# Moving half blocks of dense work within a written-out tensor-engine order: attention scores, and the tiles of a chunked recurrence

## The reference, cut to what matters

```
h   = RMSNorm(x);  c = h @ w_in            # RWKV-7 columns, attention q|k|v, two gates
A   = RWKV-7 time mixing of c              # matrix-state recurrence, 8 heads of 64
Bd  = differential attention               # softmax(q1 k1) - lam*softmax(q2 k2), times v
mix = sigmoid(gA)*(A @ w_out_a) + sigmoid(gB)*(Bd @ w_out_b)
x   = x + RMSNorm(mix @ w_o)
x   = x + RMSNorm(SwiGLU(RMSNorm(x) @ w_ffn_in) @ w_ffn_out)
```

## Time and profile before

| | |
|---|---|
| median of 3 runs | 1002.26 us (1001.57 to 1004.27) |
| the profiled execution's own time | 1004.91 us |
| its span, first to last instruction | 1003.1 us |
| busy | PE 96%, PEld 91%, POOL 55%, DVE 45%, ACT 29% |
| mean granted TensorE clock | 0.996 of 2.4 GHz |
| attention, 190 to 324 us | PE busy 130.66 of 134 us |
| recurrence, 324 to 480 us, tiles 0 to 3 | PE busy 34.78 of 39, 34.62 of 38, 35.76 of 39, 35.97 of 40 us |

### The profile page before, as it was taken

How to read it: one execution, slowest core, us unless ns; L and a number is a source line. 1 busy time by engine, 2 the same in 40 slices (tenths; PEclk the granted TensorE clock), 3 DMA queues, 4 the chain that set the end, 5 groups by cost and what they waited for, 6 DMA issues and landing times.

```text
span 1003.1 us, 23249 instructions
## 1 busy us (share of the span) xinstructions
PE 959.4 (96%) x9424; PEld 910.9 (91%) x9424; DVE 450.6 (45%) x870; ACT 290.3 (29%) x828; POOL 549.9 (55%) x595
## 2 busy tenths in 40 slices
PE   5999999999999899889999989999999999999996
PEld 4999899988878787778899989999999999999996
DVE  5456688467744445455466653333333333100003
ACT  5225265245564233432313541111111111111101
POOL 6667899634354243243469325555555555656671
PEclk9999999999999999999999999999999999999998
DMA  8333322332223111150046322223322223223232
GB/s 252 93 86 84 85 63 72 114 109 76 78 67 93 39 47 35 55 208 28 28 122 217 94 64 63 84 85 91 95 84 84 84 85 96 81 80 95 80 95 90
DMA packets 138306, 89.76 MB, mean 89 GB/s; under 512 B 5514, under 2 KB 130160, under 8 KB 138224
## 3 DMA queue, kind: packets, MB, share of 16 engines
q1 hardware_dynamic: 129604, 73.17, 25.7%
q10 hardware_dynamic: 8620, 15.42, 4.3%
HBM read 79.39 MB, written 9.19 MB: 88 GB/s over the span
## 4 chain that ended last, share of the span: by engine, by line
PE 86%; DVE 6%; ACT 4%; POOL 2%; issue 2%; DMA 1%; ACTq 0%; DVEq 0%; SPq 0%; POOLq 0%
PE dense L1069 71%; PE side L1149 3%; PE side L1192 1%; PE side L1218 1%; POOL w_lo L770 1%; PE side L1270 1%; PE side L977 1%; PE side L910 1%; DMA xs<-in_x_prompt 1%; PE side L896 1%; POOL w_hi L765 1%; PE side L951 1%; DVE gain L1731 1%; DVE h_lo L1724 0%; PE side L1242 0%
## 5 line engine op out<-in xcount | busy, mean ns | idle before, releaser
L765 POOL TENSOR_SCALAR w_hi<-w_raw 128x256 fp32r<-128x256 f32 (+1 forms) x255 | 155.6, 629 | 348.7 <-PE dense L1069 331.1
L770 POOL TENSOR_TENSOR w_lo<-w_raw,w_hi 128x256 fp32r<-128x256 f32 (+1 forms) x255 | 323.0, 1288 | 9.8
L1069 PE MATMUL dense<-h_hi,w_hi 128*128 128x272 f32 (+2 forms) x1376 | 297.8, 295 | 2.9 <-DVE h_lo L1724 1.5
L1069 PE MATMUL dense<-h_hi,w_lo 128*128 128x272 f32 (+2 forms) x1376 | 289.3, 289 | 0.0
L1069 PE MATMUL dense<-h_lo,w_hi 128*128 128x272 f32 (+2 forms) x1376 | 288.4, 288 | 0.0
L1069 PEld LDWEIGHTS dense<-h_hi,w_hi 128*128 128x128 f32 x1376 | 217.8, 189 | 12.4 <-issue 6.9
L1069 PEld LDWEIGHTS dense<-h_lo,w_hi 128*128 128x128 f32 x1376 | 218.4, 189 | 0.0
L1069 PEld LDWEIGHTS dense<-h_hi,w_lo 128*128 128x128 f32 x1376 | 217.4, 189 | 0.0
L1069 PE MATMUL dense<-S,w_hi 128*128 128x272 f32 (+2 forms) x648 | 109.3, 289 | 0.0
L1069 PEld LDWEIGHTS dense<-S,w_hi 128*128 128x128 f32 x648 | 92.1, 188 | 0.3 <-issue 0.2
L1069 PE MATMUL dense<-S,w_lo 128*128 128x272 f32 (+2 forms) x324 | 68.2, 288 | 0.0
(11 more groups left out here) (286 smaller groups left out, 1345.4 us busy)
## 6 DMA issues: line engine op xcount, KB each, us to landing
w_raw<-in_w_ffn_in SPq DMA_DIRECT2D x44, 512.0 KB, 3.8
w_raw<-in_w_in SPq DMA_DIRECT2D x43, 512.0 KB, 3.9
w_raw<-in_w_ffn_out SPq DMA_DIRECT2D x16, 448.0 KB, 3.7
gates<-gst ACTq DMA_DIRECT2D x16, 272.0 KB, 2.1
w_raw<-in_w_ffn_out SPq DMA_DIRECT2D x8, 512.0 KB, 3.8
w_raw<-in_w_out_a SPq DMA_DIRECT2D x5, 512.0 KB, 3.5
w_raw<-in_w_o SPq DMA_DIRECT2D x5, 512.0 KB, 4.5
mb<-gates ACTq DMA_DIRECT2D x1, 2176.0 KB, 9.2
```

The source lines that it names most:

```text
L765: ins = nc.gpsimd.tensor_scalar(hi[:, q], raw[:, q], 1.0, 0.0, ALU.mult, ALU.add)
L770: ins = nc.gpsimd.tensor_tensor(lo[:, q], raw[:, q], hi[:, q].bitcast(F32), ALU.subtract)
L1069: ins = pe.matmul(acc[:, bk, 0:tn], w, r[:, t0:t0 + tn], start=first and n == 0, stop=final and n == 2)
```

## The change

In attention the third piece of a head group is drawn as before, but where a group has scores (`attS`, i + 2 still in range) it goes ahead of them and behind the second piece. In the recurrence two fillers of each of the tiles 0 to 3 move: the one behind `sk` and `xi` goes ahead of `sk`, behind the transposes of `tok`; the one behind `e` goes ahead of `e`, behind `wu`. The number of pieces and what each computes are the same; tile 4 is as it was.

```diff
     for i, th in enumerate(heads):
         rows = [piece() + [("attP", *th)], piece()]
+        third = piece()
         if i + 1 < len(heads):
             rows[-1] += [("attC", *heads[i + 1])]
         if i + 2 < len(heads):
-            rows[-1] += [("attS", *heads[i + 2])]
-        rows += [piece() + [("attO", *th)] + ([("vtok", th[0] + 1)] if th[0] < SAMPLE and th[1] == 1 else [])]
+            rows[-1] += third + [("attS", *heads[i + 2])]
+            third = []
+        rows += [third + [("attO", *th)] + ([("vtok", th[0] + 1)] if th[0] < SAMPLE and th[1] == 1 else [])]
...
-        s += both("sb0", t + 1) + both("tok", t) + both("sk", t) + both("xi", t + 1) + filler(1) + scores
-        s += both("wu", t) + both("e", t) + filler(1) + yfin
+        s += both("sb0", t + 1) + both("tok", t) + filler(1) + both("sk", t) + both("xi", t + 1) + scores
+        s += both("wu", t) + filler(1) + both("e", t) + yfin
```

## The result

The changed kernel takes 1010.3 us (median of 20 runs, 1005.62 to 1016.01), the kernel before 1003.88 beside it (20 runs, 1001.57 to 1008.1): ratio 1.0066, 95% interval 1.0053 to 1.0078. It is slower by 0.66%, clear of the noise. The forecast was 1004.8 us, no difference (range 1001 to 1008). The profiled execution took 1009.32 us (span 1007.5, clock 0.994) against 1004.91 (span 1003.1, clock 0.996).

A forecast was written before the change was run, and what follows sets the result against it. The prediction took PE to bound the kernel (86% of the chain that ended last). Recurrence +1.45 us and attention +1.1 us gave +2.55 us on the median of 1002.26, so 1004.8 us, range 1001 to 1008.

The forecast's parts named there:

- I carry the difference over to the median: Whole kernel: terms counted on the profiled 1004.91 us were added to the three runs' median, 1002.26, lying 2.65 us lower.
- The clock falls once more: Rival, slower: one more stretch at 1.2 GHz, 1.7 us lost, total +4.3 us, 1006.5; chance 0.13.
- Tile 1 and tile 0: Recurrence: `sb1` g1 starts later because DVE runs `xi` ahead of `rb`'s mask; +0.95 us in tile 1, +0.5 in tile 0.
- The next thing late is DVE, and its queue holds `xi`: Recurrence, tile 1: `xi`, 1.60 us on DVE, delays `sb1` g1; cost +1.01 us net of the gain at `sk`.
- the split that delays `xi`: Rival, tile 0: POOL's split begins late and delays `xi`; +3.0 instead of +0.5 us, 1007.3 in all; chance 0.08.
- Behind `wu`: Recurrence, tile 1: 0.5 us saved at `e`, some 0.4 us of new waiting at `pre0`; -0.07 us.
- term for tile 2: Recurrence, tile 2: the delay from `sb1` is swallowed by the wait at the block's end; -0.1 us.
- Tile 3: Recurrence: `sb1` g1 is 0.64 us later, but most of it vanishes in PE's 1.4 us stall within `wu`; +0.1 us.
- I take this to end at the same moment, counted from the load: Tile 3: PE's 1.4 us stall within `wu` ends at a fixed distance from the 2 MB load, so most delay vanishes.
- Attention: Waits saved at odd heads' scores return as bank and `pT` waits at even heads; sum +1.1 us, bounds -2 and +3.
- The sample head: Attention: ACT's Exps, their scalings and the drain of `attO` come later, with `wd` standing next; +0.3 us.
- The recurrence together: Sum over tiles 0 to 3: 0.5 + 0.95 - 0.1 + 0.1 = +1.45 us, bounds -0.6 and +4.

The follow-up runs named there:

- e14_gap_xi: Kernel before with the first filler of tiles 0 to 3 behind `scores` and `xi` of the next tile behind `scores` too: 1003.11 us, ratio 0.9991.
- e13_gap: Kernel before with the first filler of tiles 0 to 3 behind `scores` instead of ahead of them, `xi` not moved: 1011.99 us, ratio 1.0077.
- e5_xi: Kernel before with only the first filler moved ahead of `sk`, and `xi` of the next tile placed behind `scores`: 1003.04 us, ratio 0.9992.
- e4_wu: Kernel before with only the second filler moved, behind `wu` and ahead of `e`: 1003.59 us, ratio 0.9996.
- e16_xi_wu_again: Repeat of the kernel before with both recurrence fillers moved and `xi` behind `scores`, attention as before: 999.94 us, ratio 0.9957.
- e11_change_again: The changed kernel run once more, unedited, beside the kernel before: 1009.54 us, ratio 1.0062.
- e1_att: Kernel before with only the attention part of the change, recurrence as before: 1005.69 us, ratio 1.0016.
- e8_prompt: Kernel before with the attention part for the prompt's heads only, sample heads and recurrence as before: 1005.78 us, ratio 1.0021.

## Why the prediction was wrong

Median to median it was 5.5 us low (1010.3 - 1004.8). By parts, which are means and so come to 5.7: 1.8 from where it started, 0.9 of work, 3.0 of clock.

**The starting point.** "I carry the difference over to the median": the three runs' 1002.26 lay 1.8 us under what 112 runs give (1004.07). The profiled execution, 1004.91, was nearer to the truth, though it held a whole fall of the clock; the mean run, by its loss of 3.25 us less some 2 at the end of the span, has less than one. With 3 runs between 1001.57 and 1004.27 neither could be known, but the range should have carried it.

**The clock: the step that failed.** The prediction let the same one fall stand on both sides and gave "The clock falls once more" 0.13. It was this rival that came, with 3.0 ±0.6 us a run against the 1.7 it was priced at: not one fall more but nearly two, so that even the rival, at 1006.5, was 3.8 us low. The sum had the clock's term at nothing, with the earlier trace rows as the only ground. Yet the forecast itself held what brings the falls: it has `sb1` g1 "waiting about 2 us" where it waited 0.19, and counts only the wait's length. The earlier trace rows was read as what follows many small matmuls and a stall; the runs show falls within or just behind single waits of 1.5 to 2.1 us, at 7 of the 12 that stand in tiles 0 and 2 of the six profiles, and none in those places in the other twelve, where the wait is under 0.8 us or gone.
The Trainium skill, TensorE: Matmul & The Clock Gate, A second HAM failure mode, says that micro-idles between groups of matmuls make the clock oscillate. It points in the right direction, but short waits alone did not do it here: `e14_gap_xi` keeps all of `sk`'s and `e`'s (2.7 us in 8 and 1.5 in 4) and loses 3.2 us, `e13_gap` has those and 6.3 us in four longer ones (1.1 to 2.1) and loses 6.1.

**Tile 1 and tile 0: right.** +0.76 and +0.47 us from one `sb0` to the next, forecast +0.95 and +0.5. (In its second profile the kernel before has tile 0 longer by 0.29 us, so +0.47 is known no better than that.) "The next thing late is DVE, and its queue holds `xi`" is what `e5_xi` shows. The second rival of the recurrence, the split that delays `xi`, did not come: the split began at 329.19, later than the 327.4 from which it was to decide, but everything ahead of it was late by 1.9 us as well, and what it waited for last was PE, not the load.

**Behind `wu`: right in kind, too small in size.** -0.07 us in tile 1 was forecast; `e4_wu` has -0.09, but so has the kernel before's own second profile (-0.10), so nothing can be told there. In tile 2 that kernel gains 1.03 us, where PE no longer waits 0.66 us for `mbd`. The prediction expected that wait still there. Its term for tile 2, -0.1 against -0.31 measured, came out near by luck: it has the delay from `sb1` swallowed, while the runs show it in full (37.89 us against 37.17 in `e4_wu`, +0.72) with the gain of 1.03 against it. Over all runs the second filler is worth -1.0 ±0.4 us.

**Tile 3: the stall is real, but not in every execution.** It sits behind the 11th matmul of `wu`, lasts 1.0 to 2.8 us in eleven profiles and is absent in seven. Timeline of `e16_xi_wu_again`, the load's issue and PE:
```profile
438.73 0.37 ACTq L1636 DMA_DIRECT2D ga<-gates  x1
442.76 0.82 PE L977 MATMUL side<-ag,xt 64*64 64x128 f32 x11
446.35 1.41 PE L977 MATMUL side<-ag,xt 64*64 64x128 f32 x21 [2.77 <-issue]
```
"I take this to end at the same moment, counted from the load" holds where it occurs: it ended 7.1 us behind this issue in the first profile of the kernel before, and 6.8 to 7.6 us behind it in the other ten, so an earlier arrival is partly swallowed (2.77 us here against 1.41). But the first profile of the changed kernel has none where the second, `e11_change_again`, has 1.0 us, and `e1_att`, whose recurrence is that of the kernel before, has none either. So the -1.36 us by which the first profiles of before and after differ in tile 3 (+0.1 forecast) are the one stall of 1.41, and say nothing of the order. The page of after lists 60 packets of kind instruction on a queue of their own; that the stall is code being loaded beside the 2 MB load was not tested.

**Attention: 2.2 ±0.3 us for 1.1 forecast.** Starts of `attO` of even heads in `e1_att`, less the kernel before's, give each pair its own price (the last one is from `e8_prompt`): +0.23, +0.46, +0.51, +0.07, -0.12, +0.13, +0.33 and +0.48 us for the prompt, against +0.2, +0.4, -0.3, +0.1, -0.1, +0.2, +0.4 and -0.1. Six of eight are within 0.1 us; the misses are tile 1's pair with `vtok`, where `attP` waited 1.01 us and not 0.8, and the saving at the scores did not make up for it, and the last prompt pair. The mechanism was the one forecast: `attP` waits for the Exp behind each `vtok`, and in tile 2 `attO` starts 1.45 us behind the even scores (244.53, 243.08) where 0.84 is free, 0.61 of new waiting against 0.75. The sample head cost 0.41, forecast 0.3.

**The recurrence together:** +1.1 ±0.4 for 1.45.

## What to carry to other kernels

Before filling a wait on the bounding engine, look at what its filler covered where it stood: here it covered 1.6 us of work of another engine that nobody needed yet, and moving that work back by one step (`xi` behind `scores`) turned +2.4 us of work into -2.4. When a forecast lengthens waits of PE, here from 0.2 or 0.7 to 1.5 us, give the clock a price of its own: here it was nearly half of the loss. And read differences of half a per cent as work time and clock loss apart: work time added up over the parts to 0.3 us, the time itself did not.

## What the runs showed of the hardware

A fall of the clock makes 1.7 us of clock loss (3.4 us at 0.50), or 3.4 in two places of `e13_gap` (6.8 us each). It is not in every execution: the kernel before had one behind tile 3 (475.6 us) in its first profile and behind the 1.7 us wait near 600 in its second, at the same mean clock of 0.996. Places that fell in some profile of some kernel: at `rb`'s waits in tiles 0 and 2 (five of the six profiles that have them), at the end of tile 3's stall where it lasted 2.2 to 2.8 us (three of four profiles), behind tile 3 (seven profiles of 18), and behind the wait near 600 (six). So one profile tells where a fall can be, and only a series of runs what it costs.
